# The attention half of a two-branch output product, made in plain fp32 inside the delta rule's first substitution

## The chip, the cores and the metric

The program runs on 1 core of a Trainium2 chip. TensorE (PE in the profile) multiplies, VectorE (DVE), ScalarE (ACT) and GpSimd (POOL) do the elementwise work, SyncE (SP) issues most of the DMAs. The metric is the device time of one execution in microseconds (us), median of several.

## The reference

Two transformer-like blocks of two layers each, D_MODEL 1024, sequence 512, all in float32. The change concerns the two layers of the first block:

```python
for l in range(DEPTH):                       # DEPTH = 2
    h = rmsnorm(x, norm_mix_g[l])
    proj = h @ w_in[l]
    ...
    y_attn = grid_attention(qa, ka, va) @ w_o_attn[l]      # (512, 512) @ (512, 1024)
    ...
    o = bidir_gated_deltanet(qd, kd, vd, beta, g)          # chunks of 64, needs inverses of (I + A)
    o = rmsnorm(o, dn_out_norm_g[l]) * jax.nn.silu(z)
    y_dn = o @ w_o_dn[l]                                   # (512, 512) @ (512, 1024)
    gates = jax.nn.sigmoid(gate_logit).reshape(b, s, 2, D_MODEL)
    mixed = gates[:, :, 0] * y_attn + gates[:, :, 1] * y_dn
    x = x + (mixed @ w_out[l])
    ...                                                    # then a convolved FFN adds to x
```

The attention output exists before the delta rule starts; its product with `w_o_attn` needs nothing of the delta rule.

## The kernel before

Everything is held transposed: a tensor of 1024 channels by 512 tokens is 8 blocks of 128 partitions by 512 columns. `X` holds x (2 MB), `ARENA` 40 such blocks (`A(i)` is block i), PSUM 8 banks of 128x512 float32 (`BANK`). The order on each engine is the order in which the code of that engine is written (`delta_pe`, `delta_act`, `delta_dve`, `delta_pool`, `gates_sp` and so on); engines meet only in semaphores. `nth(name, k)` is "the k-th event of that name in this layer".

**The dense products** (`gemm_pe`, `gemm_sp`, `split_weights`). A slab is the weight of one output block: 8 tiles of 128x128 (`KB` = 8). SP loads it into one of four slots (512 KB), POOL splits it into a high part `W_HI` (L286) and a remainder `W_LO` (L288), both fp32r, and PE does per tile three single-pass fp32r products of 128x512: high by high, high by low, low by high (L335 to L337). SP loads a slot again when PE has finished the slab in it.

**The delta rule.** After the exponentials and key products (`decays`, `keys`) 128 small triangular systems per direction are inverted in three stages. DVE does a *substitution* on 32x32 blocks: 31 pairs of small instructions (L1520, L1523) between block transposes (L1506 in, L1529 `INVERSE_ROWS` and L1533 `INVERSE_COLS` out), first for direction d = 0, then for d = 1. From each, PE and ACT in turn put the 64 and 128 blocks together (L1400, L1410, L1418, L1425, L1431 on PE, L1260 to L1287 on ACT): four pairs of heads in groups of two, for d = 0 while DVE does the second substitution, then for d = 1. Between the key products and these, PE makes `spread` (L1356, 8 groups of two plain fp32 products with 512 columns, whose results ACT exponentiates in L1248, event `gpe`) and the squares of the queries (L1381, four plain fp32 products, event `qsum`). ACT also packs the diagonal blocks for DVE (`compact`, L1209; event `diag` lets a substitution start) and takes the sigmoid of the attention gates, H (L1254). Then comes the recurrence over chunks (L1439 to L1470) and a norm (L553 to L614).

**The branch outputs** (`gates_pe`, `gates_act`, `gates_dve`). One slab holds 4 tiles of `w_o_attn` and 4 of `w_o_dn`. With `halves=True` each slab fills two banks: 4 tiles x 3 products for y_attn, then the same for y_dn. The inputs are split first: ACT makes the high parts (L451), DVE the remainders (L455), all of `branch(0..7)`, where 0 to 3 are the attention output in A(0) to A(3) and 4 to 7 the normed delta output in A(6) to A(9). For each output block DVE multiplies y_attn by its gate (L1678), y_dn by its gate (L1683) and adds (L1687). When all eight are mixed DVE splits them (L455) and PE multiplies by `w_out` (8 slabs of 8 tiles); the sum goes to X in `model_dve` (L475). With `late=True` the first two slabs are taken in two parts, so that the last tiles of the input are needed later.

Of the kernel before, what the change touches and what calls it, by code (L numbers as in the profile page):

```python
# [62 lines left out]
def build(nc, w_k8, w_k12, w_k10, xT, memT, par, cst, even, odd, outT, scratch, gate_rows):  # L63
# [4 lines left out]
    with ctx:  # L68
# [149 lines left out]
        def gemm_sp(sp, src, first, slabs, width, halves=False, after=None):  # L218
# [30 lines left out]
        def gates_sp(sp, first, l):  # L249
# [8 lines left out]
            for k in range(GATES):  # L258
# [760 lines left out]
        def wk(a, n):  # L1019
# [8 lines left out]
        PER_LAYER = dict(gate_act=5, squared=2, square_sums=2, square_roots=2, cumx=1, row_psum=1, row_lo=1, rows=1, tok_psum=4, ktok=4, vtok=4, pick_a=4, pick_v=4, diff=8,  # L1028
                         decay=8, scaled=8, kk=8, m=8, qk=8, gp=8, gpe=8, qd=8, kd=4, unit=2, inv=5, diag=4, x32_psum=8, x32=8,
                         t32_psum=8, t32=8, turn_psum=8, turn=8, x64_psum=8, x64=8, t64_psum=8, t64=8, ks=24, r=24, vn=32, vz=32,  # L1030
                         su=24, s=24, o=2, oc=4, oz=4, zero=1)

        ONE_OF = {"gate_act": ("gtok", "cum", "cum_exp", "row_hi", "rest"), "squared": ("ksq", "qsq"),
                  "square_sums": ("ksum", "qsum"), "square_roots": ("kroot", "qrow")}
# [166 lines left out]

        def delta_act(act):
# [39 lines left out]
            compact(0, PAIRS - 1, PAIRS).then_inc(dn["diag"], 1)  # L1242
            for i in range(2 * PAIRS):
# [5 lines left out]
            compact(1, 0, PAIRS).then_inc(dn["diag"], 1)  # L1249

            act.wait_ge(*nth("qsum", 1))
            nc.scalar.activation(QUERY_ROWS, BANK[6][0:64, :], ACT.Copy, scale=DN_D * DN_D * EPS).then_inc(dn["square_roots"], 1)
            for k in range(0, KB, 2):
                last = nc.scalar.activation(H[:, k * SEQ:(k + 2) * SEQ], H[:, k * SEQ:(k + 2) * SEQ], ACT.Sigmoid)  # L1254
            last.then_inc(attn_gates, 1)
# [48 lines left out]
            for k in range(4):  # L1304
                h_hi_act(k, branch_hi, branch)
            norms_done(act)

        def delta_pe(pe):
# [69 lines left out]
            pe.wait_ge(*nth("m", 2 * PAIRS))  # L1378
            pe.wait_ge(*nth("qsq", 1))
            for p in range(PAIRS):  # L1380
                last = mm(BANK[6][0:64, :], norm_pick(y_norm(l), 0, p), QUERY_SQ[p], start=p == 0, stop=p == PAIRS - 1)  # L1381
            last.then_inc(dn["square_sums"], 1)

            for d in range(2):
# [4 lines left out]
                for p in range(0, PAIRS, 2):  # L1389
                    both = [(4 * d + q, 3 * (q % 2), q) for q in (p, p + 1)]  # L1390
                    for u, b, q in both:
                        if u == 0:
                            pe.wait_ge(*nth("gpe", 2 * PAIRS))
                        elif u == 1:
                            pe.wait_ge(*nth("m", 2 * PAIRS))
# [175 lines left out]
        def delta_pool(pool):  # L1571
# [63 lines left out]
        def gates_back_sp(sp, l):  # L1635
            sp.wait_ge(dn["o"], 2 * (l + 1))
# [18 lines left out]
        def gates_act(act):  # L1655
# [5 lines left out]
            skip_banks(need_act, 2, n=2)  # L1661
# [5 lines left out]
        def gates_dve(dve, l):  # L1667
            need = need_dve
            for k in range(KB):
                h_lo_dve(dve, k, branch_lo, branch_hi, branch)  # L1670
            banks_taken(dve, need, f"gates{l}")
            dve.wait_ge(attn_gates, l + 1)
            per = {bank_full[b]: 2 for b in range(4)} | {bank_free[b]: 2 for b in range(4)} | {mixed_ready: 4, dn_gates: 2}
            with need.loop(dve, 2, per) as i:
                for nb in range(4):
                    ya, yd = 2 * (nb % 2), 2 * (nb % 2) + 1
                    dve.wait_ge(bank_full[ya], need(bank_full[ya]))
# [1604 lines left out]
```

## Time and profile before

| | |
|---|---|
| median of 3 runs | 3763.67 us (3753.75 to 3767.72) |
| the profiled execution | 3760.46 us, its span 3758.6 us |
| PE busy | 3586.9 us (95%) |
| DVE, ACT, POOL busy | 1716.3 us (46%), 978.1 us (26%), 1819.9 us (48%) |
| mean granted TensorE clock | 0.97 of full |
| the delta rule of the two layers | about 331 to 522 us and 1300 to 1491 us of the span |
| branch outputs, to the first product with `w_out` | 524 to 575 us and 1493 to 1544 us |

Times are us from the start of the span. The granted clock is 1.00 for 2.4 GHz and 0.50 for 1.2 GHz. A plain fp32 matmul appears as two matmul records; a duration of a matmul contains the drain of its pipeline, so the pace of a row of matmuls is the distance of their starts.

### The profile page before, as it was taken

What the parts mean: (1) busy time and instruction counts of PE and PEld (TensorE: products, weight loads), DVE (VectorE), ACT (ScalarE), POOL (GpSimd) and SP (SyncE); (2) the same over time, 40 slices, a digit from 0 to 9 for tenths busy, and PEclk for the clock granted to TensorE, in tenths of its full rate; (3) what the DMA queues carried; (4) which work ended last, traced back from release to release, by engine and by line L of the source; (5) the groups of instructions that cost most, each with busy time, mean ns of one, the idle gap of its engine ahead of it and who ended that gap; (6) DMA issues with size and microseconds to landing.
All of it is one profiled execution on the core that took longest, in us unless ns stands there. A gap on an engine that the chain in (4) does not pass through costs nothing.

```text
span 3758.6 us, 49965 instructions
## 1 busy us (share of the span) xinstructions
PE 3586.9 (95%) x18796; PEld 2882.4 (77%) x18796; DVE 1716.3 (46%) x2670; ACT 978.1 (26%) x1732; POOL 1819.9 (48%) x1049
## 2 busy tenths in 40 slices
PE   7999799999999979999999999999999999999999
PEld 5776677878776757787887788888888789888887
DVE  5255645737434574564551164444434124344342
ACT  3235532201223464121121133232101124232110
POOL 5522235656553222566565534435656431535654
PEclk9999799999999969999999989999999999999999
DMA  3211012323231101222222311213223423212222
GB/s 118 87 48 32 24 57 84 100 85 99 86 95 51 51 1 46 90 90 95 89 95 90 110 36 57 73 52 98 101 84 96 112 87 94 79 56 89 101 89 90
DMA packets 80743, 292.88 MB, mean 78 GB/s; under 512 B 8520, under 2 KB 9672, under 8 KB 80456
## 3 DMA queue, kind: packets, MB, share of 16 engines
q1 hardware_dynamic: 78496, 283.82, 23.7%
q10 hardware_dynamic: 1032, 2.62, 0.6%
q0 software_dynamic: 1056, 4.19, 0.3%
q8 instruction: 115, 1.88, 0.2%
q14 instruction: 44, 0.36, 0.0%
HBM read 281.69 MB, written 8.91 MB: 77 GB/s over the span
## 4 chain that ended last, share of the span: by engine, by line
PE 80%; DVE 9%; ACT 4%; issue 4%; DMA 1%; POOL 1%; DVEq 0%; ACTq 0%; SPq 0%; POOLq 0%
PE PSUM L337 19%; PE PSUM L336 19%; PE PSUM L335 19%; PE PSUM L896 2%; PE PSUM L1881 1%; PE PSUM L898 1%; PE PSUM L897 1%; DVE PSUM L494 1%; PE PSUM L1885 1%; DMA SLABS<-w_k 1%; PE PSUM L951 1%; DVE ACT_HI L1772 1%; PE PSUM L1459 1%; PE PSUM L908 1%; PE PSUM L1418 1%
## 5 line engine op out<-in xcount | busy, mean ns | idle before, releaser
L288 POOL TENSOR_TENSOR W_LOS<-SLABS,W_HI 128x1024 fp32r<-128x1024 f32 (+2 forms) x454 | 1157.7, 2550 | 37.9
L286 POOL TENSOR_SCALAR W_HI<-SLABS 128x1024 fp32r<-128x1024 f32 (+2 forms) x454 | 511.7, 1127 | 1316.6 <-DMA SLABS<-w_k 1316.6
L336 PE MATMUL PSUM<-H_LO,W_HI 128*128 128x512 f32 x2480 | 982.5, 396 | 0.0
L335 PE MATMUL PSUM<-H_HI,W_HI 128*128 128x512 f32 x2224 | 883.4, 397 | 26.1 <-DVE H_LO L479 20.9
L337 PE MATMUL PSUM<-H_HI,W_LOS 128*128 128x512 f32 x2224 | 884.7, 398 | 0.0
L336 PEld LDWEIGHTS PSUM<-H_LO,W_HI 128*128 128x128 f32 x2480 | 467.7, 189 | 118.2 <-issue 2.4
L335 PEld LDWEIGHTS PSUM<-H_HI,W_HI 128*128 128x128 f32 x2224 | 419.0, 188 | 131.8 <-issue 21.9
L337 PEld LDWEIGHTS PSUM<-H_HI,W_LOS 128*128 128x128 f32 x2224 | 418.5, 188 | 98.1
L494 DVE TENSOR_TENSOR PSUM<-PSUM,FACTORS 128x512 f32<-128x512 f32 x282 | 195.2, 695 | 554.0 <-PE PSUM L337 491.4
L335 PE MATMUL PSUM<-ACT_HI,W_HI 128*128 128x512 f32 x928 | 370.5, 399 | 13.0 <-DVE H_LO L455 6.4
L337 PE MATMUL PSUM<-ACT_HI,W_LOS 128*128 128x512 f32 x928 | 372.0, 401 | 0.0
L336 PE MATMUL PSUM<-ACT_LO,W_HI 128*128 128x512 f32 x896 | 356.2, 398 | 0.0
L335 PEld LDWEIGHTS PSUM<-ACT_HI,W_HI 128*128 128x128 f32 x928 | 176.5, 190 | 57.2 <-issue 7.9
L337 PEld LDWEIGHTS PSUM<-ACT_HI,W_LOS 128*128 128x128 f32 x928 | 176.1, 190 | 41.5
L336 PEld LDWEIGHTS PSUM<-ACT_LO,W_HI 128*128 128x128 f32 x896 | 169.9, 190 | 42.9 <-issue 0.2
L475 DVE TENSOR_TENSOR X<-PSUM,X 128x512 f32<-128x512 f32 x72 | 49.7, 690 | 206.9 <-PE PSUM L337 206.9
L402 DVE TENSOR_TENSOR X<-PSUM,X 128x512 f32<-128x512 f32 x40 | 27.7, 691 | 248.8 <-PE PSUM L337 248.8
L423 ACT ACTIVATE H_HI<-X,PARAM 128x512 fp32r<-128x512 f32 x64 | 45.6, 723 | 258.2 <-DVE X L475 258.2
L335 PE MATMUL PSUM<-H_LO,W_HI 128*128 128x512 f32 x256 | 102.1, 399 | 7.9 <-DVE ACT_HI L455 7.9
L896 PE MATMUL PSUM<-H_HI,W_HI 128*128 128x512 f32 x256 | 109.3, 427 | 0.0
L1753 DVE SCALAR_TENSOR_TENSOR QF<-PSUM,PARAM,QF 128x511 f32<-128x511 f32 (+1 forms) x88 | 66.0, 750 | 88.2 <-ACT QF L1723 42.5
L898 PE MATMUL PSUM<-H_HI,W_LOS 128*128 128x512 f32 x256 | 103.3, 404 | 0.0
(499 smaller groups left out, 5048.5 us busy)
## 6 DMA issues: line engine op xcount, KB each, us to landing
SLABS<-w_k SPq DMA_DIRECT2D x422, 512.0 KB, 3.5
SLABS<-w_k SPq DMA_DIRECT2D x32, 768.0 KB, 4.3
SLABS<-w_k SPq DMA_DIRECT2D x32, 640.0 KB, 3.9
ARENA<-gate_rows SPq DMA_DIRECT2D x8, 512.0 KB, 5.2
bias_rows<-SQ ACTq DMA_DIRECT2D x1, 2560.0 KB
X<-xT SPq DMA_DIRECT2D x1, 2048.0 KB, 8.4
gate_rows<-RT SPq DMA_DIRECT2D x8, 256.0 KB, 2.1
DX<-bias_rows POOLq DMA_DIRECT2D x8, 256.0 KB, 3.0
```

The source lines that it names most:

```text
L286: nc.gpsimd.tensor_scalar(hi, raw, 1.0, 0.0, MUL, ADD).then_inc(pool_step, 1)
L288: nc.gpsimd.tensor_tensor(lo, raw, hi.bitcast(F), SUB).then_inc(slab_split[s], 1)
L335: mm(out, w_hi, rhs[0](k), start=k == first, stop=False)
L336: mm(out, w_hi, rhs[1](k), start=False, stop=False)
L337: last = mm(out, w_lo, rhs[0](k), start=False, stop=k == final - 1)
L423: nc.scalar.activation(hi(k), blk(X, k), ACT.Copy, scale=G(gain, k)).then_inc(h_hi, 1)
L475: nc.vector.tensor_tensor(xb, BANK[k % 4][:], xb, ADD).then_inc(bank_free[k % 4], 1)
L494: nc.vector.tensor_tensor(BANK[b][:], BANK[b][:], FACTORS[:], MUL).then_inc(scaled, 1)
L896: mm(BANK[b][:], hi, blk(H_HI, i), start=i == 0, stop=False)
L897: mm(BANK[b][:], hi, blk(H_LO2, i), start=False, stop=False)
L898: last = mm(BANK[b][:], lo, blk(H_HI, i), start=False, stop=i == KB - 1)
L1753: last = nc.vector.scalar_tensor_tensor(buf[:, lo:hi], BANK[b][:, lo + o:hi + o], G(conv, col), buf[:, lo:hi], MUL, ADD)
```

## The change

The attention half is taken out of the branch product and made earlier, in plain fp32 with the unsplit weights, which lie in `X` while x is away; each result block then replaces the weights that made it. In more detail, per layer:

- While the gate products run (`gates_sp`), SP stores X to DRAM (`x_rows`, second layer only; the first has it in `xT`) and loads the 8 attention halves of the weights into X (one DMA of 2 MB).
- On PE, 8 products `early(j)`, each 4 plain fp32 matmuls of 128x512 in banks 4 to 7, stand between the key products and `spread`; the squares of the queries move up between `early(3)` and `early(4)`, into bank 0.
- ACT copies each result into X (`keep(j)`); the sigmoid of the gates and the second packing move up among them, the exponentials of `spread` come after the last `keep`.
- After its decays POOL multiplies H by X, four instructions of 128x1024 (event `gated`), then SP loads x back into X.
- The branch product has slabs of 4 tiles (256 KB, 12 matmuls each, one bank per slab), POOL splits half as much for it, ACT and DVE split only branch blocks 4 to 7, and DVE has two instructions per output block instead of three.

```diff
-        def gemm_sp(sp, src, first, slabs, width, halves=False, after=None):
+        def gemm_sp(sp, src, first, slabs, width, halves=False, after=None, skipped=0):
...
                 sp.dma_start(SLAB[s][:, 0:width * P],
-                             src[bass.ds(i * SLOTS + (first + s), 1)].rearrange("o p n -> (o p) n")).then_inc(slab_in[s], 16)
+                             src[bass.ds(i * SLOTS + (first + s), 1), :, skipped * P:(skipped + width) * P].rearrange("o p n -> (o p) n")
+                             ).then_inc(slab_in[s], 16)
...
+                if k == SLOTS - 1 and l:
+                    sp.dma_start(x_rows, X[:]).then_inc(x_in, 16)
+                if k == 2 * SLOTS - 1:
+                    if l:
+                        sp.wait_ge(x_in, weights_there(l) - 16)
+                    sp.dma_start(X[:].rearrange("p (j c) -> p j c", j=KB), w_k8[first + GATES:first + GATES + KB, :, 0:4 * P].rearrange("j p c -> p j c")
+                                 ).then_inc(x_in, 16)
...
+            def keep(j):
+                act.wait_ge(*nth(f"early{j}", 1))
+                nc.scalar.activation(blk(X, j), BANK[early_bank(j)][:], ACT.Copy).then_inc(dn["square_roots"], 1)
+
+            keep(0)
+            for k in range(0, KB, 2):
+                last = nc.scalar.activation(H[:, k * SEQ:(k + 2) * SEQ], H[:, k * SEQ:(k + 2) * SEQ], ACT.Sigmoid)
+            last.then_inc(attn_gates, 1)
+            for j in range(1, 4):
+                keep(j)
+            act.wait_ge(*nth("qsum", 1))
+            nc.scalar.activation(QUERY_ROWS, BANK[0][0:64, :], ACT.Copy, scale=DN_D * DN_D * EPS).then_inc(dn["square_roots"], 1)
+            compact(1, 0, PAIRS).then_inc(dn["diag"], 1)
+            for j in range(4, KB):
+                keep(j)
             for i in range(2 * PAIRS):
...
                 nc.scalar.activation(qdec(p, d), BANK[i % 4][:], ACT.Exp).then_inc(dn["gpe"], 1)
-            compact(1, 0, PAIRS).then_inc(dn["diag"], 1)
...
+            def early(j):
+                if j < 4:
+                    pe.wait_ge(*nth("m", 6 if j < 2 else 8))
+                else:
+                    pe.wait_ge(*nth(f"kept{j - 4}", 1))
+                for k in range(4):
+                    last = mm(BANK[early_bank(j)][:], tl(blk(X, j), k), A(k), start=k == 0, stop=k == 3)
+                last.then_inc(dn["square_sums"], 1)
+
+            pe.wait_ge(x_in, weights_there(l))
+            for j in range(4):
+                early(j)
+            pe.wait_ge(*nth("decay", 2 * PAIRS))
+            pe.wait_ge(*nth("qsq", 1))
+            for p in range(PAIRS):
+                last = mm(BANK[0][0:64, :], norm_pick(y_norm(l), 0, p), QUERY_SQ[p], start=p == 0, stop=p == PAIRS - 1)
+            last.then_inc(dn["square_sums"], 1)
+            for j in range(4, KB):
+                early(j)
+            pe.wait_ge(*nth("qrow", 1))
             for i in range(2 * PAIRS):
                 spread(i)
...
+            pool.wait_ge(attn_gates, delta_l[0] + 1)
+            pool.wait_ge(*nth(f"kept{KB - 1}", 1))
+            for k in range(0, KB, 2):
+                both = slice(k * SEQ, (k + 2) * SEQ)
+                last = nc.gpsimd.tensor_tensor(H[:, both], H[:, both], X[:, both], MUL)
+            last.then_inc(dn["zero"], 1)
...
-            gemm_pe(pe, 8, (branch_hi, branch_lo), halves=True, ready=h_split, late=True)
+            gemm_pe(pe, 8, (lambda k: branch_hi(4 + k), lambda k: branch_lo(4 + k)), kb=4, ready=h_split, late=True)
...
+            sp.wait_ge(dn["zero"], 2 * (l + 1))
+            if l:
+                sp.dma_start(X[:], x_rows).then_inc(x_in, 16)
+            else:
+                sp.dma_start(X[:].rearrange("p (k n) -> p k n", k=KB), xT.rearrange("(k p) n -> p k n", p=P)).then_inc(x_in, 16)
...
-            for k in range(KB):
+            for k in range(4, KB):
                 h_lo_dve(dve, k, branch_lo, branch_hi, branch)
...
-                split_weights(pool, 2 * KB, first=lambda s: pool.wait_ge(*nth("o", 1 if s < 2 else 2)))
+                split_weights(pool, KB, 4, first=lambda s: pool.wait_ge(*nth("o", 1 if s < 2 else 2)))
+                split_weights(pool, KB)
```

PE behind the key products of the first layer, before: `spread` (CONST is the spreading weight, ROWS_R the rows), the squares, and the first small products of the d = 0 chain.

```order
L1330 MATMUL PSUM<-ARENA 128x128 x8
L1356 MATMUL PSUM<-ROWS_R,CONST 64x512 x16
L1381 MATMUL PSUM<-SLABS,CONST 64x512 x2
L1381 MATMUL PSUM<-SQ,CONST 64x512 x2
L1400 MATMUL PSUM<-SLABS,ARENA 32x32 x32
```

The same place now:

```order
L1356 MATMUL PSUM<-ARENA 128x128 x8
L1409 MATMUL PSUM<-ARENA,X 128x512 x16
L1418 MATMUL PSUM<-SLABS,CONST 64x512 x2
L1418 MATMUL PSUM<-SQ,CONST 64x512 x2
L1409 MATMUL PSUM<-ARENA,X 128x512 x16
L1382 MATMUL PSUM<-ROWS_R,CONST 64x512 x16
L1442 MATMUL PSUM<-SLABS,ARENA 32x32 x32
```

32 new products (two lots of 16) stand in front of `spread`, and the squares stand between the lots; the line numbers are those of the changed file.

ACT at the same place, before, from the squaring of the queries to the start of the d = 0 chain:

```order
L1240 ACTIVATE SQ<-ARENA 128x512 x2
L1209 ACTIVATE SLABS<-ARENA 32x256 x4
L1248 ACTIVATE ARENA<-PSUM 128x512 x4
L1248 ACTIVATE SCAN<-PSUM 128x512 x2
L1248 ACTIVATE SLABS<-PSUM 128x512
L1248 ACTIVATE VTOK<-PSUM 128x512
L1209 ACTIVATE SLABS<-ARENA 32x1024 x4
L1252 ACTIVATE FACTORS<-PSUM 64x512
L1254 ACT_TABLE_LOAD
L1254 ACTIVATE H<-H 128x1024 x4
L1260 ACTIVATE ARENA<-SLABS 32x32x32 x4
```

And now:

```order
L1265 ACTIVATE X<-PSUM 128x512
L1269 ACT_TABLE_LOAD
L1269 ACTIVATE H<-H 128x1024 x4
L1265 ACTIVATE X<-PSUM 128x512 x3
L1274 ACTIVATE FACTORS<-PSUM 64x512
L1228 ACTIVATE SLABS<-ARENA 32x1024 x4
L1265 ACTIVATE X<-PSUM 128x512 x4
L1283 ACT_TABLE_LOAD
L1283 ACTIVATE ARENA<-PSUM 128x512 x4
L1283 ACTIVATE SCAN<-PSUM 128x512 x2
L1283 ACTIVATE SLABS<-PSUM 128x512
L1283 ACTIVATE VTOK<-PSUM 128x512
```

The eight exponentials (L1248, now L1283) have moved from the front of this stretch to its end, just ahead of the packing L1260, and the sigmoid in the middle makes a second table load necessary.

## Rows read from the trace of the kernel before

**Rows 1.** The page: busy time of the engines, us (share) and instructions.

```profile
PE 3586.9 (95%) x18796; PEld 2882.4 (77%) x18796; DVE 1716.3 (46%) x2670; ACT 978.1 (26%) x1732; POOL 1819.9 (48%) x1049
```

**Rows 2.** Stretches: length, busy us per engine (count), PEclk, DMA share, GB/s.

```profile
362.50:366.20 3.70, 3.65 (x16) 1.03 (x16) 2.40 (x3) 3.65 (x5) 3.60 (x4) 1.00 0.00 0
366.20:370.20 4.00, 0.00 (x1) 0.01 (x1) 0.74 (x2) 3.94 (x10) 0.00 (x0) 0.99 0.00 0
370.20:380.50 10.30, 10.30 (x20) 2.66 (x21) 9.41 (x27) 6.32 (x10) 0.00 (x0) 0.51 0.00 1
397.00:424.00 27.00, 21.85 (x356) 20.60 (x357) 24.84 (x65) 14.65 (x28) 1.10 (x2) 0.50 0.01 2
428.00:440.00 12.00, 8.38 (x177) 7.76 (x177) 2.35 (x2) 8.98 (x15) 12.00 (x12) 0.72 0.01 3
```

**Rows 3.** Timeline of PE around the first substitution, first layer.

```profile
362.52 3.65 PE L1356 MATMUL PSUM<-ROWS_R,CONST 64*64 64x512 f32 x16
370.20 7.09 PE L1356 MATMUL PSUM<-ROWS_R,CONST 64*64 64x512 f32 x16 [4.03 <-ACT ARENA L1248]
380.51 1.88 PE L1381 MATMUL PSUM<-SQ,CONST 128*64 128x512 f32 x4
396.97 1.92 PE L1400 MATMUL PSUM<-SLABS,ARENA 32*32 32x32 f32 x64 [14.58 <-DVE SLABS L1529]
```

**Rows 4.** Timeline of ACT in the same stretch and at the second direction.

```profile
367.85 1.67 ACT L1209 ACTIVATE SLABS<-ARENA 32x256 f32<-32x256 f32 x4
377.95 4.25 ACT L1209 ACTIVATE SLABS<-ARENA 32x1024 f32<-32x1024 f32 x4
382.43 0.59 ACT L1252 ACTIVATE FACTORS<-PSUM 64x512 f32<-64x512 f32 x1 [0.22 <-PE PSUM L1381]
383.04 1.28 ACT L1254 ACT_TABLE_LOAD   x1
384.33 3.90 ACT L1254 ACTIVATE H<-H 128x1024 f32<-128x1024 f32 x4
398.74 4.25 ACT L1260 ACTIVATE ARENA<-SLABS 32x1024 f32<-32x1024 f32 x4 [10.51 <-DVE SLABS L1533]
428.63 4.25 ACT L1260 ACTIVATE ARENA<-SLABS 32x1024 f32<-32x1024 f32 x4
456.60 0.59 ACT L1287 ACTIVATE ARENA<-PSUM 64x512 f32<-64x512 f32 x1 [0.34 <-PE PSUM L1431]
```

**Rows 5.** Timeline of DVE: the ends of the two substitutions.

```profile
394.90 2.01 DVE L1529 STREAM_TRANSPOSE SLABS<-SLABS 128x1024 f32<-128x1024 f32 x1
425.79 1.87 DVE L1533 STREAM_TRANSPOSE SLABS<-SLABS 128x1024 f32<-128x1024 f32 x1
```

**Rows 6.** Timeline of PE in the branch product, first layer.

```profile
523.95 0.47 PE L335 MATMUL PSUM<-H_LO,W_HI 128*128 128x512 f32 x1 [2.27 <-DVE ACT_HI L455]
535.19 0.39 PE L335 MATMUL PSUM<-H_LO,W_HI 128*128 128x512 f32 x1
535.42 0.40 PE L336 MATMUL PSUM<-ACT_HI,W_HI 128*128 128x512 f32 x1
571.35 0.40 PE L337 MATMUL PSUM<-H_LO,W_LOS 128*128 128x512 f32 x1
574.88 0.76 PE L335 MATMUL PSUM<-ACT_HI,W_HI 128*128 128x512 f32 x1 [3.13 <-DVE H_LO L455]
```

**Rows 7.** The adds of the mixing: count, shortest/median/longest ns, first and last start.

```profile
L1687 DVE TENSOR_TENSOR H<-QF,KF x16: 692/1126/2455, 536.7 to 1542.0; 128x512 f32 x16
```

**Rows 8.** Busy time by line, POOL, 512.8 to 527.6: four slabs.

```profile
L288 POOL TENSOR_TENSOR W_LOS<-SLABS,W_HI 128x1024 fp32r<-128x1024 f32 x4 | 9.7, 2434 | 0.3
L286 POOL TENSOR_SCALAR W_HI<-SLABS 128x1024 fp32r<-128x1024 f32 x4 | 4.6, 1155 | 0.0
```

**Rows 9.** Timeline of POOL in the recurrence; in brackets its idle time before.

```profile
484.75 2.49 POOL L1622 TENSOR_TENSOR ARENA<-ARENA 128x512 f32<-128x512 f32 x2 [38.58 <-ACT ARENA L1302]
```

**Rows 10.** The page's DMA issues: count, KB each, median us to landing.

```profile
SLABS<-w_k SPq DMA_DIRECT2D x422, 512.0 KB, 3.5
```

More of the change, by code:

```diff
@@ L1026, in build @@
         delta_l = [None]
-        PER_LAYER = dict(gate_act=5, squared=2, square_sums=2, square_roots=2, cumx=1, row_psum=1, row_lo=1, rows=1, tok_psum=4, ktok=4, vtok=4, pick_a=4, pick_v=4, diff=8,
+        PER_LAYER = dict(gate_act=5, squared=2, square_sums=10, square_roots=10, cumx=1, row_psum=1, row_lo=1, rows=1, tok_psum=4, ktok=4, vtok=4, pick_a=4, pick_v=4, diff=8,
                          decay=8, scaled=8, kk=8, m=8, qk=8, gp=8, gpe=8, qd=8, kd=4, unit=2, inv=5, diag=4, x32_psum=8, x32=8,
                          t32_psum=8, t32=8, turn_psum=8, turn=8, x64_psum=8, x64=8, t64_psum=8, t64=8, ks=24, r=24, vn=32, vz=32,
-                         su=24, s=24, o=2, oc=4, oz=4, zero=1)
+                         su=24, s=24, o=2, oc=4, oz=4, zero=2)
         ONE_OF = {"gate_act": ("gtok", "cum", "cum_exp", "row_hi", "rest"), "squared": ("ksq", "qsq"),
-                  "square_sums": ("ksum", "qsum"), "square_roots": ("kroot", "qrow")}
+                  "square_sums": ("ksum", *(f"early{j}" for j in range(4)), "qsum", *(f"early{j}" for j in range(4, KB))),
+                  "square_roots": ("kroot", *(f"kept{j}" for j in range(4)), "qrow", *(f"kept{j}" for j in range(4, KB))),
+                  "zero": ("zero", "gated")}
         def nth(name, k):
@@ L1200, in build, with weights_there, x_there, early_bank @@
         INVERSE_ROWS, INVERSE_COLS, TURNED_IN, DIAG_BLOCKS = (1, 4), (2, 5), 3, (3, 4)
+        def weights_there(l):
+            return 80 if l else 32
+        def x_there(l):
+            return weights_there(l) + 16
+        def early_bank(j):
+            return 4 + j % 4
         def delta_act(act):
@@ L1248, in delta_act @@
                 nc.scalar.activation(qdec(p, d), BANK[i % 4][:], ACT.Exp).then_inc(dn["gpe"], 1)
-            compact(1, 0, PAIRS).then_inc(dn["diag"], 1)
[L1251 to L1255, printed above, removed]
             for d in range(2):
@@ L1303, in delta_act @@
             norms_act(act, y_norm(l))
-            for k in range(4):
-                h_hi_act(k, branch_hi, branch)
             norms_done(act)
@@ L1345, in queries @@
                 else:
-                    pe.wait_ge(*nth("qrow", 1))
+                    pe.wait_ge(*nth(f"kept{KB - 1}", 1))
                 products(p, 6, 6)
@@ L1375, in delta_pe @@
                 keys(p)
+            def early(j):
[17 more added lines that the diff above has]
+            pe.wait_ge(*nth("qrow", 1))
             for i in range(2 * PAIRS):
                 spread(i)
[L1378 to L1382, printed above, removed]
             for d in range(2):
@@ L1394, in delta_pe @@
                         elif u == 1:
-                            pe.wait_ge(*nth("m", 2 * PAIRS))
+                            pe.wait_ge(*nth(f"kept{KB - 1}", 1))
                         elif q >= 2 or d:
@@ L3040, in _ @@
                 gates_dve(dve, l)
+                dve.wait_ge(x_in, x_there(l))
                 model_dve(dve, f"ffn_g{l}", tile_of(H_HI), tile_of(H_LO2))
@@ L3112, in _ @@
                     else:
-                        gemm_sp(sp, w_k8, at, slabs, KB, halves, (lambda: gates_back_sp(sp, n)) if halves else
-                                (lambda: mem_sp(sp)) if n == 3 and slabs == OD_SLABS and at == od_first else None)
+                        gemm_sp(sp, w_k8, at, slabs, 4 if halves else KB, False, (lambda: gates_back_sp(sp, n)) if halves else
+                                (lambda: mem_sp(sp)) if n == 3 and slabs == OD_SLABS and at == od_first else None, 4 if halves else 0)
                     at += slabs
@@ L3278 @@
     gate_rows = nc.dram_tensor("gate_rows", (KB, P, SEQ), f, kind="Internal").ap()
-    build(nc, *args, out, scratch, gate_rows)
+    x_rows = nc.dram_tensor("x_rows", (P, KB * SEQ), f, kind="Internal").ap()
+    build(nc, *args, out, scratch, gate_rows, x_rows)
     r = _run(nc, [arrays], core_ids=[0])
```

23 lines of the change are left out of this document (9 added, 14 removed).

## Prediction

> **What bounds the kernel now.** I read the page first: PE is busy 95% of the span, every other engine about half or less [rows 1]. So nearly everywhere the time is the pace of PE's matmuls, and the exceptions are the delta rules, where PE waits. Then the timeline of PE around the branch product: from the first matmul at 523.95 to the last at 571.35 there are 192 fp32r matmuls, two neighbours 0.23 us apart, and the first product with `w_out` follows at 574.88, 3.53 us after the start of the last, because DVE must first mix and split the last block [rows 6]. 192 x 0.233 = 44.7 of the 47.4 us: this stretch is bound by PE, with about 2.7 us of stalls at its start, where PE waits for the remainders of the inputs (L455).
>
> Then the delta rule. In the first layer PE has nothing between the squares' last starts after 380.51 and the first block product at 396.97: it idles 14.58 us for the transposed result of the first substitution, and before that 4.03 us for ACT, which is packing blocks while `spread`'s banks wait for their exponentials [rows 3]. DVE is the path there: the first substitution's `INVERSE_ROWS` comes at 394.90 + 2.01 = 396.91 and the second substitution ends at 425.79 + 1.87 = 427.66 [rows 5]. Beside the second one runs the d = 0 chain of PE and ACT, and ACT takes the next direction's packing up at 428.63 [rows 4]: DVE and the d = 0 chain end within 1 us of each other. So the gap before 396.97 is free for PE, but what is late after it has only some room: the clock and 1 us decide. The second layer repeats all of this.
>
> **The branch product.** Half of its matmuls go: 96 x 0.233 = 22.4 us per layer. What stays is 95 x 0.233 = 22.1 us from the first to the last start, and the same 3.53 us from the last start to the first of `w_out` (one multiply, one add, one split), so 25.7 us in place of 574.88 - 523.95 = 50.9 [rows 6]. The start does not move: ACT and DVE can split the delta output only when it is normed, and before, too, DVE's first split came directly behind the last norm multiply. The stalls of 2.7 us mostly go, since DVE has four blocks to split instead of eight and POOL is soon out of its way: per slab POOL takes 1.16 + 2.43 = 3.6 us now and about half of that for 4 tiles, four slabs in 7 instead of 14 us [rows 8].
>
> New stalls are possible at the other end. PE takes 12 x 0.233 = 2.8 us per slab instead of 5.6, and behind it stand three things. Weights: a slot is loaded when PE leaves it, three slabs or 8.4 us ahead of need; a 512 KB load lands in 3.5 us [rows 10] and the split takes 3.6 or, half, 1.8: 7.1 us at most, so hidden, with 1.3 us left for the first full slabs of `w_out`. DVE: one multiply of about 0.69 and one add of 1.13 in the median, 2.46 at worst [rows 7], plus 0.2 between them: 2.0 us as a rule against 2.8, hidden, but 3.35 at worst, not hidden. And POOL now runs without a pause through the full slabs of `w_out` while DVE splits the mixed blocks; the adds beside it show what that does to an instruction of DVE with two SBUF operands (0.69 alone, up to 2.46) [rows 7]. I put 1.5 us per layer for it and 0.5 for what is left of the first stalls; bounds 0 and 5. Saving: 50.9 - 25.7 - 2.0 = 23.2 us per layer, bounds 20.2 and 25.2.
>
> **The early products.** One plain fp32 matmul of 512 columns is two records; four records of the squares take 1.88 us including a drain of about 0.6, so starts are 0.43 apart and a matmul takes 0.86 us at full clock [rows 3]. 32 of them are 27.5 us, more than the 22.4 removed, and more than the 14.58 us gap. But `spread` and the squares moved behind them, so the whole row on PE counts. The key products end at 362.5 where before `spread` starts [rows 3]. `early(0..3)` 13.8, squares 3.4, `early(4..7)` 13.8: 362.6 + 31.0 = 393.6. The waits in it are met: m(8), the second packing and the sigmoid are off its way, ACT's chain behind 369.5 being one copy 0.6, table 1.28, sigmoid 3.90, three copies, the squares' copy at 380, the packing 4.25 to about 385, copies [rows 4], each far ahead of the bank it frees. Then `spread`: four groups take 3.65 us at full clock [rows 3], eight 7.3, to 400.9, ACT's exponentials (about 0.6 each, as the copy in [rows 4]) one behind, so the first block product starts at about 401.8 instead of 396.97, 4.8 us late. The sigmoid now leaves ACT with another function table, so the exponentials need a load of 1.28 us [rows 4]; it falls into the first groups of `spread`, from 394.2. The Trainium skill ("ScalarE: Activation LUTs", "What ACT_TABLE_LOAD costs") gives about 2.66 us for a switch, drain included; here the sigmoid starts 1.29 us after the start of its table load, so the trace does not show the drain, and by the page's figure the load would end at 396.9 and push the block product by about 1 us more.
>
> ACT packs d = 0 (L1260) from 401.7 instead of 398.74, 3.0 us late, to 406.0. From there the chain is PE and ACT in turn. Before, from 402.99 to 428.63, it took 25.6 us, with the clock at 1.2 GHz from 397 to 424 after the 14.6 us of idleness [rows 2, 3]. The same chain for d = 1, with a clock of 0.72 on average over its first 12 us [rows 2], went from 432.88 to 457.19, 24.3 us, and had three key-query products of 1.1 to 1.5 us in it [rows 4]. PE now comes to it from 39 us of unbroken work, so I take d = 1's pace without those three: 21 us, end at 427.0, just inside DVE's 427.66. Then ACT starts on d = 1 at 427.7 instead of 428.63: a gain of 0.9. If PE ran it at 1.2 GHz all through, it would end at 431.6, a loss of 3.0. I take 0 per layer, nearest to d = 1's row.
>
> **The rest, at nothing.** The 2 MB loads and the store ride on a DMA system that is three quarters idle in the gate products, where each slot has three slabs of slack; if that cover failed, one load of 2 MB is four of 512 KB at 3.5 us, 14 us once. POOL's four products of 128x1024 with two operands cost 4 x 2.43 = 9.7 us [rows 8] out of 38.58 us in which it waited [rows 9]. The reload of X is due at 587, more than 100 us later. DVE waits for `gated` and for x in front of work that comes long after.
>
> **The sum.** 2 x 23.2 = 46.4 us off the profiled 3760.46 us (span 3758.6 and 1.9 around it): 3714. The median of the runs shown is 3.2 us above that execution; between the two I say 3715.
>
> **Rivals.**
> 1. As summed, 0.78: 3715, by the bounds of its terms (2 x 20.2 less 2 x 3.0; 2 x 25.2 plus 2 x 0.9) from 3708 to 3729.
> 2. The mixing on DVE or the weights become the pace of the branch product, 0.08. At 3.35 us per slab DVE needs 8 x 0.55 = 4.4 us more per layer and the splitting behind it 3 more: 3730. For it the longest add [rows 7], against it its median.
> 3. The d = 0 chain stays at 1.2 GHz and sets the path, 0.07: 2 x 3 to 2 x 4 us, 3722. For it, 3.5 us of idleness will again stand behind the first block products (ACT's packing), and before, such a gap lowered the clock for d = 1 too [rows 2].
> 4. Slower: the early products run at 1.2 GHz, 0.04. In the trace four groups of `spread` took 3.65 us and the next four 7.09, after 4.03 us without a matmul, with the clock at 0.51 over 10.3 us of dense plain fp32 [rows 2, 3]. If PE came to `early(0)` with such a gap and stayed low, 38 us of work would become 76: the block product starts 43 us late, 41 us of it through the packing, and 2 x 41 - 46 = 36 us are lost: 3798. It would decide from about six tenths of the stretch at 1.2 GHz on. Against it: the clock was 1.00 at 362.5 to 366.2 [rows 2] and no gap is left. The Trainium skill ("TensorE: Matmul & The Clock Gate", "What's actually happening") has the half-rate clock as the default state, which activity releases; by that rule the new dense work holds the clock up, and the trace before, whose clock fell only behind a gap, agrees.
> 5. The change frees PE and the time is not saved, as PE's removed work only turns into another wait, 0.03: between 3735 and 3765.
>
> **How the numbers follow.** A difference of 0.5% (19 us) is about what a measurement can tell from no change. Cases 1 to 3 are faster by more: 0.93. Case 5 gives 0.03 for the same, case 4 0.04 for slower. The range of 8 in 10 takes the likeliest case and most of 2 and 3: 3705 to 3730.
>
> **What would show it.** In the changed profile: 32 plain matmuls per layer at 0.43 us per record, clock 1.00 from 362 to 401; the first block product (now L1442) near 401.8; ACT's second packing of diagonals for d = 1 at 427.7, give or take 4; the branch product 26 to 29 us from its first matmul to the first of `w_out`; adds on DVE in steps of 2.8 us. Wrong would be: `early(0)` waiting for the weights or for a bank, a clock of 0.5 in it, PE waiting for POOL's split in the branch product, or a pause of more than 6 us before `w_out`.

## The result, and the profile after

The changed kernel takes 3733.94 us, median of 8 runs, against 3758.16 for the kernel before, median of 8: a ratio of 0.993, 95% interval 0.9915 to 0.9946. Forecast were 3715 and 3705 to 3730. The gain is there, but it is 24 us and not 46. The profiled execution took 3725.19 us (span 3723.4), 35.3 under that of before. Medians here and below are of fast runs; one later run of the changed kernel, 4460.11 us at a mean granted clock of 0.741, is left out.

Four stretches, the same in every trace, show where the time went. A: the first matmul with `KR` in a delta rule to the first of the branch product. B: from there to the first of `w_out`. C: from there to the first statistic of the next RMS norm (DVE, `SQ<-PSUM,CONST 128x128`). D: from that norm to the next, the feed-forward stage, which the change does not touch. Times in us, first and second layer:

| kernel | A | B | C | D |
|---|---|---|---|---|
| before | 183.26, 183.35 | 50.93, 51.00 | 54.25, 54.25 | 373.61, 378.34 |
| changed | 186.71, 182.67 | 29.70, 29.33 | 58.37, 58.65 | 378.87, 373.22 |

B gave 42.9 us in all, of the 50.5 that a B of 25.7 us in each layer would give. C took back 8.5 and A 2.8: 31.6 us remain of 46.4. D nets to nothing here, and outside these stretches the changed kernel's profile is 3.7 us shorter.

**The early products** ran as forecast. The page, one row of the windows (columns as in [rows 2]) and the timeline of PE in the first delta rule:

```profile
PE 3585.1 (96%) x18732; PEld 2866.8 (77%) x18732; DVE 1694.3 (46%) x2646; ACT 986.7 (26%) x1742; POOL 1818.3 (49%) x1057
```

```profile
362.00:401.00 39.00, 38.45 (x104) 15.08 (x104) 32.31 (x73) 26.86 (x39) 4.46 (x6) 1.00 0.00 0
404.00:424.00 20.00, 17.59 (x280) 16.80 (x281) 18.32 (x50) 10.91 (x24) 0.00 (x0) 0.50 0.01 2
```

```profile
361.96 13.97 PE L1409 MATMUL PSUM<-ARENA,X 128*128 128x512 f32 x32 [0.21 <-DVE ARENA L1544]
...
379.44 14.00 PE L1409 MATMUL PSUM<-ARENA,X 128*128 128x512 f32 x32
393.37 7.08 PE L1382 MATMUL PSUM<-ROWS_R,CONST 64*64 64x512 f32 x32
401.24 0.95 PE L1442 MATMUL PSUM<-SLABS,ARENA 32*32 32x32 f32 x49 [0.79 <-ACT VTOK L1283]
...
406.21 1.92 PE L1452 MATMUL PSUM<-SLABS 32*32 32x32 f32 x64 [3.77 <-ACT SLABS L1296]
```

64 records in 27.97 us, PE without a gap at a granted clock of 1.00 (2.4 GHz), where before it idled 14.58 us [rows 3]; the first block product starts at 401.24. Then PE idles 3.77 us for ACT's packing, and the clock is 0.50 (1.2 GHz) from 404 to 424. ACT's second packing of the diagonals starts 431.16, 3.5 us later than forecast, against 428.63 before [rows 4], and the first KR matmul is 0.8 us earlier than before.

**The branch product.** PE at its two ends, first layer:

```profile
526.63 0.76 PE L343 MATMUL PSUM<-H_LO,W_HI 128*128 128x512 f32 x1 [2.34 <-DVE ACT_HI L463]
527.20 0.63 PE L344 MATMUL PSUM<-ACT_HI,W_HI 128*128 128x512 f32 x1
527.62 0.63 PE L345 MATMUL PSUM<-H_LO,W_LOS 128*128 128x512 f32 x1
...
539.78 0.50 PE L343 MATMUL PSUM<-H_LO,W_HI 128*128 128x512 f32 x1 [0.27 <-POOL W_LOS L296]
...
550.62 0.40 PE L344 MATMUL PSUM<-ACT_HI,W_HI 128*128 128x512 f32 x1
550.85 0.40 PE L345 MATMUL PSUM<-H_LO,W_LOS 128*128 128x512 f32 x1
556.33 0.77 PE L343 MATMUL PSUM<-ACT_HI,W_HI 128*128 128x512 f32 x1 [5.09 <-DVE H_LO L463]
...
559.01 0.80 PE L343 MATMUL PSUM<-ACT_HI,W_HI 128*128 128x512 f32 x1 [1.06 <-DVE H_LO L463]
...
563.23 0.79 PE L343 MATMUL PSUM<-ACT_LO,W_HI 128*128 128x512 f32 x1 [1.13 <-DVE H_LO L463]
```

Behind the first step of 0.57 us, the first eight start 0.42 to 0.43 us apart, not 0.23: 1.2 GHz. The pause before `w_out` is 5.09 us in place of 3.13 [rows 6], and two more of 1.06 and 1.13 follow, each for a split of a mixed block. Before, there was one such pause:

```profile
580.23 0.50 PE L335 MATMUL PSUM<-ACT_LO,W_HI 128*128 128x512 f32 x1 [0.76 <-DVE H_LO L455]
```

The clock behind the first product with `w_out` was low for longer, too. Windows (columns as in [rows 2]) of the changed kernel, then of before:

```profile
556.33:567.30 10.97, 8.78 (x19) 5.67 (x20) 9.25 (x7) 0.58 (x2) 6.21 (x3) 0.50 0.00 0
```

```profile
574.88:578.30 3.42, 3.42 (x8) 2.77 (x9) 3.42 (x4) 1.12 (x2) 2.82 (x2) 0.50 0.00 0
```

What DVE did before `w_out` in the changed kernel, and POOL beside it:

```profile
549.53 1.34 DVE L1735 TENSOR_TENSOR H<-H,KF 128x512 f32 x1
551.40 0.69 DVE L1732 TENSOR_TENSOR KF<-PSUM,ARENA 128x512 f32<-128x512 f32 x1 [0.53 <-PE PSUM L345]
552.24 2.50 DVE L1735 TENSOR_TENSOR H<-H,KF 128x512 f32 x1
554.95 4.00 DVE L463 TENSOR_TENSOR H_LO<-H,ACT_HI 128x512 fp32r<-128x512 f32 x2 [0.21 <-DVE H L1735]
558.88 6.70 DVE L463 TENSOR_TENSOR H_LO<-H,ACT_LO 128x512 fp32r<-128x512 f32 x6
```

```profile
550.29 1.49 POOL L294 TENSOR_SCALAR W_HI<-SLABS 128x1024 fp32r<-128x1024 f32 x1
551.86 2.34 POOL L296 TENSOR_TENSOR W_LOS<-SLABS,W_HI 128x1024 fp32r<-128x1024 f32 x1
554.16 1.49 POOL L294 TENSOR_SCALAR W_HI<-SLABS 128x1024 fp32r<-128x1024 f32 x1
555.73 2.67 POOL L296 TENSOR_TENSOR W_LOS<-SLABS,W_HI 128x1024 fp32r<-128x1024 f32 x1
```

The multiply with one operand in PSUM took 0.69 us for each of the eight blocks, beside POOL or not. The add with both operands in SBUF, issued at 552.24 just after POOL's subtraction began at 551.86, ends at 554.74, some 0.5 us after it: 2.50 us. POOL has no pause here from 537.42 to 562.6, since PE now frees a slot every 2.8 us.

### The profile page after: what moved, and what is told of

Same layout as the page of the kernel before. It is cut to its first block, busy times and chain, and to the rows that moved or that the text cites. A ratio compares the mean times of both kernels' runs of the same rounds, so it can differ in the third digit from the quotient of the medians.

```text
span 3723.4 us, 49812 instructions
## 1 busy us (share of the span) xinstructions
PE 3585.1 (96%) x18732; PEld 2866.8 (77%) x18732; DVE 1694.3 (46%) x2646; ACT 986.7 (26%) x1742; POOL 1818.3 (49%) x1057
## 3 DMA queue, kind: packets, MB, share of 16 engines
q1 hardware_dynamic: 81904, 290.11, 23.9%
## 4 chain that ended last, share of the span: by engine, by line
PE 80%; DVE 9%; ACT 4%; issue 3%; DMA 2%; POOL 1%; DVEq 0%; ACTq 0%; SPq 0%; POOLq 0%
PE PSUM L345 19%; PE PSUM L344 19%; PE PSUM L343 19%; PE PSUM L904 2%; PE PSUM L1929 1%; PE PSUM L905 1%; PE PSUM L906 1%; PE PSUM L1933 1%; DVE PSUM L502 1%; DMA SLABS<-w_k 1%; PE PSUM L959 1%; DVE ACT_HI L1820 1%; PE PSUM L1501 1%; PE PSUM L916 1%; PE PSUM L1409 1%
## 5 line engine op out<-in xcount | busy, mean ns | idle before, releaser
L296 POOL TENSOR_TENSOR W_LOS<-SLABS,W_HI 128x1024 fp32r<-128x1024 f32 (+3 forms) x454 | 1142.1, 2516 | 37.9
L294 POOL TENSOR_SCALAR W_HI<-SLABS 128x1024 fp32r<-128x1024 f32 (+3 forms) x454 | 507.6, 1118 | 1299.7 <-DMA SLABS<-w_k 1299.6
L344 PEld LDWEIGHTS PSUM<-ACT_LO,W_HI 128*128 128x128 f32 x896 | 169.8, 190 | 42.9 <-issue 0.2
L410 DVE TENSOR_TENSOR X<-PSUM,X 128x512 f32<-128x512 f32 x40 | 27.6, 691 | 248.3 <-PE PSUM L345 248.3
```

What stands on the lines that cost most here:

```text
L294: nc.gpsimd.tensor_scalar(hi, raw, 1.0, 0.0, MUL, ADD).then_inc(pool_step, 1)
L296: nc.gpsimd.tensor_tensor(lo, raw, hi.bitcast(F), SUB).then_inc(slab_split[s], 1)
L344: mm(out, w_hi, rhs[1](k), start=False, stop=False)
```

## The experiments

Theory A: POOL's long subtractions block DVE instructions with two SBUF operands, and PE's pauses for DVE lower the clock. Theory B: the pauses are DVE's own chain. Theories C to F stand with their experiments. The kernels are variants of the changed one unless said otherwise; a median stands beside that of the kernel before on the same chip.

**copied_lo**: POOL copies, instead of subtracting, for the w_out slabs (shortened: the wait for the high part goes too, and the other slabs keep the subtraction).

```
...
-  nc.gpsimd.tensor_tensor(lo, raw, hi.bitcast(F), SUB)
+  nc.gpsimd.tensor_scalar(lo, raw, 1.0, 0.0, MUL, ADD)
...
```

> Work left out: for the eight w_out slabs POOL no longer subtracts (two SBUF operands) but copies the raw slab into the remainder (one operand); the product of the weights' remainder is therefore not the reference's. Theory A (POOL's two-operand subtraction blocks DVE instructions that have two SBUF operands): the last add before w_out falls from 2.5 us to about 0.7 to 1.3, the stretch from the first branch matmul to the first of w_out from 29.5 to about 27.5 us, the stretch from there to the next norm's first DVE step from 58.4 to about 54.5 (54.25 before), in both layers. Theory B (the pause before w_out is DVE's own chain, and the slower w_out only the clock that falls in it): 29.5 and 58.4 stay within 0.5 us.

One run, 3719.63 us (before 3757.05). B 28.00 and 28.33, C 54.52 and 54.52 (before: 54.25). So all but 0.3 us of C's loss hangs on POOL's instruction and not on DVE's own chain; theory B falls. What stays in B is mostly its slow start: the clock is low there as in the changed kernel. The copy is also shorter than the subtraction (1.48 us), so this run does not tell the kind of POOL's instruction from its length. The last add took 1.32 us, not 0.7: it was issued at 552.70, behind the start of a one-operand instruction of POOL (552.44, 1.04 us), and such a one delays it too.

**psum_add**: the product stays in its PSUM bank, and the add reads it there (shortened: the semaphores are left out).

```
...
-  tensor_tensor(KF[:], BANK[nb][:], A(i * 4 + (10 + nb)), MUL)
-  tensor_tensor(blk(H, i * 4 + nb), blk(H, i * 4 + nb), KF[:], ADD)
+  tensor_tensor(BANK[nb][:], BANK[nb][:], A(i * 4 + (10 + nb)), MUL)
+  tensor_tensor(blk(H, i * 4 + nb), blk(H, i * 4 + nb), BANK[nb][:], ADD)
...
```

> The same computation: the multiply with the sigmoid writes into its PSUM bank and the add reads it there, so the add has one SBUF operand and one in PSUM; the bank is free after the add instead of after the multiply. Theory A: the add is not blocked by POOL any more: 0.7 us in place of up to 2.5, branch to w_out 29.5 to about 28, w_out to the norm 58.4 to about 57.5 (the splits of the mixed blocks still have two SBUF operands and stay blocked): 2 to 3 us per layer, 5 in all. Theory B: nothing over 0.5 us per layer.

3727.37 us (4 runs; before 3757.05). B 25.57 and 27.22, better than expected, C 57.26 and 57.29. Nearly all of the 1.65 us between the two layers is the clock at the start of B, low in the second layer and not in the first, which the edit does not touch; the pause before `w_out` is 2.92 and 3.03 us in place of 5.09 and 5.14. DVE's adds and the first splits:

```profile
549.49 0.69 DVE L1735 TENSOR_TENSOR H<-H,PSUM 128x512 f32 x1
551.35 0.70 DVE L1732 TENSOR_TENSOR PSUM<-PSUM,ARENA 128x512 f32<-128x512 f32 x1 [1.17 <-PE PSUM L345]
552.20 0.69 DVE L1735 TENSOR_TENSOR H<-H,PSUM 128x512 f32 x1
553.20 2.22 DVE L463 TENSOR_TENSOR H_LO<-H,ACT_HI 128x512 fp32r<-128x512 f32 x2 [0.30 <-DVE H L1735]
```

The same add, the same place, one operand moved to PSUM: 0.69 in place of 2.50 us. The Trainium skill ("SBUF — State Buffer", "Who interferes with whom") states this rule: an instruction of DVE with two SBUF inputs contends with one of GpSimd that reads SBUF, one with at most one SBUF input, outside DVE's 2-port modes, does not, and the port pair that the two share is an exclusive lock. The traces agree: the add with two SBUF inputs took 2.50 us and ended 0.5 us after POOL's subtraction, with one input in PSUM 0.69, and copied_lo's one-operand copy delayed a two-input add to 1.32.

**halved_tt** and **halved_256**: POOL's subtraction in pieces of 512, then 256 columns, everywhere (shown for 512).

```
...
-  nc.gpsimd.tensor_tensor(lo, raw, hi.bitcast(F), SUB).then_inc(slab_split[s], 1)
+  for c in range(0, width * P, 512):
+      piece = slice(c, min(c + 512, width * P))
+      last = nc.gpsimd.tensor_tensor(lo[:, piece], raw[:, piece], hi.bitcast(F)[:, piece], SUB)
+  last.then_inc(slab_split[s], 1)
...
```

> The same computation: POOL's subtraction of a slab is cut into pieces of 512 columns (two or three instructions in place of one) everywhere. Theory A, first form (DVE is blocked to the end of the POOL instruction that runs): a blocked DVE instruction waits at most about 1.3 us in place of 2.5 to 3.8: branch to w_out 28.5, w_out to the norm 56.5, and the feed-forward stages' long wait for the split of the hidden block (4 to 5 us, in one of the first layer's two parts in either profile) goes, so norm to norm 373.3 both times. Second form (DVE waits until POOL has no two-operand work ready): 29.5 and 58.4 stay, the feed-forward waits too, and POOL's extra instructions can only cost: 0 to 5 us slower.

3692.97 us (4 runs), ratio to before 0.9832 (0.9806 to 0.9859): 41 us under the changed kernel. The first form of theory A holds: every D is 372.2, and the pause before `w_out` is 4.22 and 4.33 us. Not all 41 us are POOL's blocking itself, though: in the profiles B and C give 10 of them, A 7 and D 8, and the clock was high at the start of B in both layers, behind the same wait of 2.34 us:

```profile
517.57 0.47 PE L346 MATMUL PSUM<-H_LO,W_HI 128*128 128x512 f32 x1 [2.34 <-DVE ACT_HI L466]
517.88 0.39 PE L347 MATMUL PSUM<-ACT_HI,W_HI 128*128 128x512 f32 x1
518.11 0.40 PE L348 MATMUL PSUM<-H_LO,W_LOS 128*128 128x512 f32 x1
```

> The changed kernel with POOL's subtractions in pieces of 256 columns (four to six instructions a slab) instead of 512. Theory A (DVE waits to the end of the POOL instruction that runs): a DVE split waits at most about 0.65 us instead of 1.3, branch to w_out 26.9 to about 26, w_out to norm 56.1 to about 55.2: 3 to 4 us under halved_tt, 3689. Rival: the more pieces, the more start-up on POOL, and the fuller POOL is the more often DVE meets it: POOL's slab takes 0.2 to 0.5 us longer and nothing is gained: 3693 to 3697.

3691.36 us (4 runs; before 3757.87), ratio 0.9816 (0.9797 to 0.9836): the same within the noise, but B and C move as expected:

| kernel | A | B | C | D |
|---|---|---|---|---|
| halved_tt | 181.14, 181.27 | 26.86, 26.97 | 56.09, 56.09 | 372.21, 372.21 |
| halved_256 | 181.23, 181.27 | 25.60, 26.17 | 54.12, 54.12 | 372.21, 372.22 |

In halved_256, DVE, POOL and PE at the end of the branch product:

```profile
542.84 0.69 DVE L1738 TENSOR_TENSOR H<-H,KF 128x512 f32 x1
543.73 2.06 DVE L466 TENSOR_TENSOR H_LO<-H,ACT_HI 128x512 fp32r<-128x512 f32 x2 [0.21 <-DVE H L1738]
```

```profile
541.78 1.04 POOL L294 TENSOR_SCALAR W_HI<-SLABS 128x1024 fp32r<-128x1024 f32 x1
542.90 4.62 POOL L298 TENSOR_TENSOR W_LOS<-SLABS,W_HI 128x256 fp32r<-128x256 f32 x4
```

```profile
544.80 0.47 PE L346 MATMUL PSUM<-ACT_HI,W_HI 128*128 128x512 f32 x1 [2.96 <-DVE H_LO L466]
```

POOL pays, 4.62 us for a slab's subtraction in place of 2.34 (2.84 for the slab at 554.65, where DVE has no such work), and DVE gets in between the pieces; the pause is 2.96 us, 3.53 in the second layer, and PE comes out of it at 2.4 GHz, though in the first layer the clock falls for 3.4 us from 1.4 us later on. PE does not wait for the slower POOL in B or C.

**before_halved**: the same edit (512) on the kernel before.

> The kernel before, with POOL's subtraction cut into pieces of 512 columns, as in halved_tt. Theory A (the change's missing 22 us went to DVE's waits for POOL's long subtractions and to the clock that fell in them, in the branch product and behind it, where the change made POOL's work dense): cutting the pieces is worth less here than on the changed kernel, since only the feed-forward and gate stages have such waits: about 20 us, 3737; the difference between the changed kernel and this one, both with short pieces (3693 there), is then about the forecast 46 us. Theory B (the short pieces help both kernels alike, and the change itself is worth only its 24 us): 3717.

3747.64 us (12 runs; before 3758.34), ratio 0.9977 (0.9967 to 0.9987). 10.7 us, half of what I expected of it; so short pieces are worth 41 us on the changed kernel and 11 on the one before. The change itself is worth 3747.6 - 3693.0 = 54.7 us when both have short pieces (53.4 when each is taken against before on its own chip). Its stretches: A 181.66, 181.36; B 50.96, 50.84; C 54.16, 54.16; D 372.21, 372.22. Against halved_tt, A to C give 44.7 us, and with halved_256's B and C 50.6: the 46.4 of the forecast lie between. The other 10 of the 54.7 lie outside these stretches, in places where two traces do the same work with the same waits and another granted clock: one such stage takes 146.33 us in before_halved and 141.57 in halved_tt, with one wait of 1.51 us and one of 0.6 in either. The largest part, 5.3 us, lies between the first layer's D and the second delta rule: 307.34 us in before_halved, 302.05, 302.13 and 303.23 in the three profiles of the changed kernel with short pieces. Three of three may be more than chance; the cause is open.

**halved_wout**: the pieces only for the eight full w_out slabs.

> The changed kernel with short pieces only for the eight full w_out slabs of either layer. Theory A: what the change lost behind the branch product comes back there alone: branch to w_out 29.5 to about 27, w_out to norm 58.4 to 56.1, 10 us in all, about 3723; gate and feed-forward stages and the delta rule as in the changed kernel. Theory B: the gain of short pieces comes from the other stages, under 4 us here.

3729.27 us (4 runs, 3717.9 to 3733.1; before 3758.34). C 56.07 and 56.07 as expected; B 28.57 and 28.81, a miss: the clock at its start stays low. 6.5 us for both layers instead of 10.

**halved_psum**: both edits.

> Both edits: short pieces everywhere and the mixed block's add with one operand in PSUM. Theory A: adds of up to 1.4 us become 0.7, so branch to w_out 26.9 to about 26, w_out to norm 56.1 unchanged: 1 to 2 us under halved_tt, 3691. If it shows nothing, the adds are off PE's path by now: 3693.

3694.82 us (5 runs). B 25.88 and 25.96, C 56.06 and 56.06, as expected; the 2 us do not show in the total beside a spread of 6.

**warm**: 14 matmuls of no use where PE waits for the first packing, to test the clock.

```
...
+  if p == 0:
+      for _ in range(14):
+          mm(BANK[5][:], KR[:, 0:P], KR[:, 0:SEQ], start=True, stop=True)
...
```

> The same computation plus work of no use: 14 fp32r matmuls of a constant, 128x512, into an unused PSUM bank between the first block products and the wait for their evacuation, for either direction (3.8 us at 2.4 GHz). Theory C (the d = 0 chain goes slowly in the first layer since the 3.8 us pause for ACT's packing lowers the clock): the granted clock stays at 1.0 behind it, keys to ACT's second packing falls from 91.2 (first layer) and 87.0 (second) to 86.5 or less in both, keys to the recurrence from 119.9 and 114.3 to 112 to 114. Rival D (the chain's pace is ACT's and the semaphores'): at most 1 us gained; and if the 14 matmuls run at 1.2 GHz they take 7 us, 3 more than the pause: up to 3 us per direction lost.

3732.79 us (4 runs; before 3757.05): no gain clear of the noise. Windows of it, columns as above, and the second one in the changed kernel:

```profile
401.00:412.00 11.00, 10.34 (x171) 9.02 (x164) 10.11 (x27) 8.96 (x17) 0.00 (x0) 1.00 0.01 3
456.00:472.00 16.00, 16.00 (x75) 12.78 (x75) 4.03 (x18) 3.77 (x15) 0.00 (x0) 0.50 0.47 164
```

```profile
456.00:472.00 16.00, 15.30 (x149) 12.73 (x147) 6.28 (x22) 6.08 (x20) 0.00 (x0) 1.00 0.59 198
```

Theory C is right as far as it goes: the clock stays 1.00, the block chain of d = 0 ends before DVE's substitution, and the packing for d = 1 comes 87.32 and 87.10 us after the first KR matmul instead of 91.24 and 87.00. But the clock then falls to 0.50 in the recurrence, where in the changed kernel it was 1.00 from 456 to 472, and A becomes 190.84 and 190.63. Why it falls there stays open.

**early_quarter**: three of four early matmuls left out.

> Work left out: three of the four matmuls of each early product (24 of 32 per layer, 20.6 us of PE at 0.86 each), so half the branch is not the reference's. If the early products are hidden but for the 4 us that the first block product came late (401.2 instead of 397.0), the first block product comes at about 397 again and the stretch keys to branch is shorter by 0 to 4 us: DVE's substitution sets it. If they stand on the path, it is shorter by up to 20 us per layer. The clock may tell a third story: PE then waits about 12 us before the block products and they run at 1.2 GHz as before.

One run, 3719.73 us. A 183.54 and 182.57 against 186.71 and 182.67: 20.6 us of PE's work a layer are worth 3.2 and 0.1. The early products are hidden; what they cost is the start of the d = 0 chain 5 us later, and, as far as two layers of one run can tell, only where that chain runs at 1.2 GHz.

**before_look1 to 3**: the kernel before, profiled three more times.

> The kernel before, profiled again, for the two feed-forward stages: each has one place where PE waits either 4 to 5 us (norm to norm 378 to 379 us) or under 1 (373 to 374). In the changed kernel and its variants with long POOL subtractions it was long in 10 of 12 looks, in the one profile of before in 1 of 2. Theory E (the change makes the long wait more frequent, which is where the medians lose some 7 us against the two first profiles): long in at most 2 of the 6 stages of these three looks. Theory F (it is as frequent before): long in 4 to 6 of 6.

> As the first look: the kernel before, profiled again; theory E: at most 2 of 6 stages with the long wait over the three looks, theory F: 4 to 6.

> As the first look: the kernel before, profiled again; theory E: at most 2 of 6 stages with the long wait over the three looks, theory F: 4 to 6.

D was 378.72, 378.85; 373.45, 373.29; 373.52, 373.19: long in 2 of 6, in 3 of 8 with the first profile. This is the long form in the changed kernel, on DVE, POOL and PE:

```profile
751.45 3.78 DVE L1822 TENSOR_TENSOR ACT_LO<-VF,ACT_HI 128x512 f32 x1
```

```profile
751.13 3.55 POOL L296 TENSOR_TENSOR W_LOS<-SLABS,W_HI 128x1536 fp32r<-128x1536 f32 x1
```

```profile
764.04 0.80 PE L343 MATMUL PSUM<-ACT_HI,W_HI 128*128 128x512 f32 x1 [4.27 <-DVE ACT_LO L1822]
```

One split behind one subtraction of 3.55 us is followed by an idle PE of 4.27 us, which comes back at 1.2 GHz. DVE's split started 0.32 us after POOL's subtraction.

**before_ffn, after_ffn, after_again**: short pieces for the feed-forward slabs alone, on either kernel, and the changed kernel once more.

> The kernel before, with POOL's subtractions in pieces of 512 columns for the feed-forward slabs alone. Its two feed-forward stages then have no long wait, as before_halved shows (372.2 us norm to norm instead of 373.4, or 378.7 in 3 of 8 looks): about 6 us under the kernel before, 3752.

> The changed kernel with the same edit. Theory E (the change makes the feed-forward's long wait for POOL more frequent: 10 of 12 looks against 3 of 8): about 12 us under the changed kernel, 3721, and the difference to before_ffn is 29 to 32 us, as the touched stages alone give between the first two profiles (31.5). Theory F (it is equally frequent and the median's 24 us are what the change is worth): 6 us gained here too, 3728, and the difference stays at 24 us.

> The changed kernel itself, timed on the same chip beside the two others. Theory E: its difference to before is about 24 us again while after_ffn and before_ffn are 29 to 32 apart. Should the difference here come out at 30, the first median of 8 runs was chance and nothing is left to explain.

Medians 3750.19 (12 runs), 3722.62 (6) and 3731.93 (5), before 3755.74 (17): gains of 5.6 and 9.3 us where 6 and 12 were expected, and a difference of 27.6 between the two kernels, between theory E's 29 to 32 and F's 24: it decides for neither. The changed kernel is again 24 us under before. With after_again D was long in 11 of 14 stages of the changed kernel and its variants with long subtractions there, against 3 of 8 before. But the changed kernel by itself was long in 2 of 4, and the variants differ in other places. In the first layer it is 7 of 7 against 1 of 4, in the second 4 of 7 against 2 of 4. That the long wait is more frequent with the change is suggested, not shown. In after_again A was 186.71 and 186.25: the second layer's 182.67 in the first profile is one of two outcomes, and the commoner one: copied_lo, psum_add, halved_wout and after_ffn, which leave the delta rule as it is, have 182.9 to 183.1 there.

## Why the prediction was wrong

The sum lost 22 us between 46 and 24; the time is off by 19, as the forecast also started 3 us above the later median of before.

1. *The branch product's matmuls*: right. 96 matmuls go, and halved_256 has B at 25.60 and 26.17, where the bare sum said 25.7.
2. *"I put 1.5 us per layer for it and 0.5 for what is left of the first stalls; bounds 0 and 5"*: this step failed. Measured are 3.8 us per layer in B over 25.7 and 4.3 in C, 8.1 in place of 2.0. I had taken the adds' longest duration of before [rows 7], 2.46 us, for a rare case against a median of 1.13, and charged DVE's delay alone. With the change POOL runs without a pause just when the last add and the first splits stand on PE's path; in both profiles of the changed kernel the pause was 4.9 to 5.3 us in either layer. The parts, first layer: in B 1.96 us (5.09 instead of 3.13), 0.3 where PE waited for POOL's split of a slab, in that one layer only (a thing that I had named as a sign of being wrong), and 8 x 0.19 = 1.5 for the first matmuls at 1.2 GHz; in C 1.4 us more of pauses (1.06 + 1.13 against 0.76) and, as the remainder, 2.7 us of matmuls at 1.2 GHz behind them. That the pauses and C's loss come from POOL's instruction is shown by copied_lo, psum_add and the pieces: with 256 columns B and C lose nothing. The 1.5 us at B's start are another matter. POOL is idle there, and PE's wait just before, 2.34 us, is the same in halved_tt, where the clock was 1.00. The kernel before had this slow start too, in 3 of its 8 profiled layers, and it cost next to nothing: B 51.00 to 51.14 with it, 50.76 to 51.02 without, since PE stood waiting there for DVE's splits anyway. The change took those waits away, and the clock counts. So the 0.5 for "what is left of the first stalls" was 1.5, in 4 of 4 layers of the two profiles; why the clock is low there in some executions is open.
3. *The early products*: right, in place, length and clock; early_quarter shows them hidden. Rival 4, the slower one, did not come about. The drain that would have added 1 us to the table load did not show: the first exponential started 1.29 us after the load (394.09 to 395.38).
4. *"I take 0 per layer" for the delta rule*: rival 3 came true in the first layer, +3.45 us against its 3.0, and in the second it was -0.7 in one profile and +2.9 in the other. The clock fell behind the 3.77 us pause, as that rival said, but for 23.9 us in the first layer and for 6.8 at first in the second. So the d = 0 chain behind the packing took 25.7 us in the first and 20.5 in the second, where ACT then waited 1.50 us for DVE: the 21 that I had taken was right for one layer of the two. With short pieces A is the same with and without the change, 181.2 against 181.5: there my 0 was right.
5. *"The rest, at nothing"*: the loads, the store and POOL's four products were. The feed-forward stages may have lost: (11/14 - 3/8) x 2 x 5.4 us, about 4 us on average, with the variants counted, and 1 us with the changed kernel alone, 2 of 4; an estimate from few looks.
6. *Rival 2* had the right place and the wrong mechanism: DVE's steps stay at 2.7 us per slab (adds from 546.83 to 549.53) and hide; only the last add and what follows it stand on the path.

Points 2 and 4, read from traces, make 12.2 and 3: 15 of the 22 us. Point 5 may add 1 to 4. The rest, 3 to 6 us, is open, and no trace shows it: both profiled executions of the changed kernel, 3725.19 and 3724.87 us, lie 7 to 9 us under its medians, so the traces hold only part of what the medians lost. The 10 us outside the stretches between before_halved and halved_tt are open too. Single profiles of the kernel before differ by 8 us outside the stretches, from 2424.6 to 2433.0, so such a difference between two profiles proves little.

## What to carry to other kernels

When an edit makes one engine's pauses go away, look at who shared those pauses: here POOL's splitting had been spread over 51 us and became dense over 29, and the last add and the splits, DVE instructions with two SBUF operands, then met it. Price such a meeting by the longest row if it stands on the path, and add the clock that PE loses behind the pause. A wait can also hide a slow stretch of the clock: when the edit removes the wait, that stretch starts to count. Where they meet on the path, long two-operand instructions on POOL are worth cutting, or their DVE partner worth giving a PSUM operand, even where POOL itself gets slower: halved_256 beats both kernels, by 1.8% and 1.1%.

## What the hardware showed

POOL's subtraction of 128x1024 takes 2.34 to 2.71 us whole and 4.62 in four pieces beside DVE's splits. A wait of 1.5 to 2.3 us on PE had matmuls at 1.2 GHz behind it in some executions and not in others: B started low in the changed kernel and high in halved_tt behind the same 2.34 us. One stage took 141.5 or 146.3 us, another 298 or 302, in traces whose waits over 0.5 us are the same to 0.4 us. Behind the pause of 5 us before `w_out` the clock was low in all four layers of the changed kernel's two profiles. And filling one pause with useless matmuls was followed by a slow stretch elsewhere.
